# Stationary operands of the float32r matmuls laid out with a stride of two elements

## The reference, cut to what matters

```python
h = rmsnorm(x, lw['norm1_w']) * (1.0 + scale1) + shift1
proj = jnp.einsum('btd,dc->btc', h, lw['w_in'])            # 1024 -> 2304
...
s = jnp.einsum('bkgqd,bskd->bkgqs', qblk, k) * scale       # attention scores
p = jax.nn.softmax(s, axis=-1)
o = jnp.einsum('bkgqs,bskd->bkgqd', p, v)                  # attention values
...
out = jnp.einsum('btc,cd->btd', jnp.concatenate([att, ret], axis=-1), lw['w_out'])
...
gates, idx = lax.top_k(aff.transpose(0, 2, 1), cap)        # experts choose tokens
a = jnp.einsum('becd,edf->becf', xg, lw['w_gate'])
u = jnp.einsum('becd,edf->becf', xg, lw['w_up'])
y = jnp.einsum('becf,efd->becd', jax.nn.silu(a) * u, lw['w_down'])
```

## Time before, and the profile before

| | us |
|---|---|
| median of 3 runs | 3144.37 |
| lowest and highest of them | 3141.43, 3145.56 |
| the profiled execution | 3139.49 |
| its span, first to last instruction | 3137.8 |
| PE busy | 2974.2 |
| PEld busy | 2739.5 |
| DVE busy | 1852.7 |
| ACT busy | 1674.1 |
| POOL busy | 700.5 |

### The profile page before, as it was taken

How to read it: one execution, slowest core, us unless ns; L and a number is a source line. 1 busy time by engine, 2 the same in 40 slices (tenths; PEclk the granted TensorE clock), 3 DMA queues, 4 the chain that set the end, 5 groups by cost and what they waited for, 6 DMA issues and landing times. The chain is left out here.

```text
span 3137.8 us, 57856 instructions
## 1 busy us (share of the span) xinstructions
PE 2974.2 (95%) x20880; PEld 2739.5 (87%) x20880; DVE 1852.7 (59%) x3261; ACT 1674.1 (53%) x3227; POOL 700.5 (22%) x878
## 2 busy tenths in 40 slices
PE   8999997899999999999899969999999999999996
PEld 5888886688888888888788759999999999999996
DVE  5222225788888888888643387655555555555555
ACT  4222223677777777777534336544444454454454
POOL 1333335632323223232000011111111111111104
PEclk9999999999999999999899959999999999999998
DMA  7211116501010010010164336666666666666657
GB/s 256 84 68 68 68 60 203 178 14 35 17 30 20 17 33 17 20 30 17 45 208 148 120 96 201 188 194 189 194 197 189 196 196 189 191 199 195 194 184 285
DMA packets 320130, 394.76 MB, mean 126 GB/s; under 512 B 30260, under 2 KB 276488, under 8 KB 319016
## 3 DMA queue, kind: packets, MB, share of 16 engines
q1 hardware_dynamic: 307416, 356.18, 34.5%
q0 software_dynamic: 12240, 36.77, 4.8%
q10 hardware_dynamic: 384, 0.62, 0.1%
HBM read 319.60 MB, written 74.06 MB: 125 GB/s over the span
## 5 line engine op out<-in xcount | busy, mean ns | idle before, releaser
L2877 DVE TENSOR_TENSOR e_w_lo<-e_raw,e_w_hi 128x2048 fp32r<-128x2048 f32 x189 | 433.1, 2291 | 411.7 <-ACT e_w_hi L2794 411.7
L92 PE MATMUL e_ps<-e_x_hi,e_w_hi 128*128 128x272 f32 x2048 | 601.6, 294 | 2.6 <-issue 2.6
L94 PE MATMUL e_ps<-e_x_hi,e_w_lo 128*128 128x272 f32 x2048 | 593.4, 290 | 0.0
L93 PE MATMUL e_ps<-e_x_lo,e_w_hi 128*128 128x272 f32 x2048 | 590.0, 288 | 0.0
L1709 DVE TENSOR_TENSOR a_pT_lo<-a_ps_t,a_pT_hi 128x512 fp32r<-128x512 f32 (+1 forms) x648 | 367.8, 600 | 137.2 <-ACT a_pT_hi L1618 136.9
L1618 ACT ACTIVATE a_pT_hi<-a_ps_t 128x512 fp32r<-128x512 f32 (+1 forms) x648 | 319.3, 532 | 160.2 <-PE a_ps_t L1486 155.1
L92 PEld LDWEIGHTS e_ps<-e_x_hi,e_w_hi 128*128 128x128 f32 x2048 | 386.3, 189 | 3.0 <-issue 3.0
L93 PEld LDWEIGHTS e_ps<-e_x_lo,e_w_hi 128*128 128x128 f32 x2048 | 387.0, 189 | 0.0
L94 PEld LDWEIGHTS e_ps<-e_x_hi,e_w_lo 128*128 128x128 f32 x2048 | 385.8, 188 | 0.0
L2794 ACT ACTIVATE e_w_hi<-e_raw 128x2048 fp32r<-128x2048 f32 x189 | 360.6, 1908 | 0.0
L1486 PE MATMUL a_ps_t<-ident,a_prob 128*128 128x128 f32 x2184 | 329.6, 280 | 29.9 <-DVE a_pT_lo L1709 19.1
(11 more groups left out here) (358 smaller groups left out, 5492.3 us busy)
## 6 DMA issues: line engine op xcount, KB each, us to landing
e_raw<-in_w_gate SPq DMA_DIRECT2D x64, 1024.0 KB, 5.0
e_raw<-in_w_up SPq DMA_DIRECT2D x64, 1024.0 KB, 5.0
e_raw<-in_w_down SPq DMA_DIRECT2D x64, 1024.0 KB, 5.0
s_ret<-p_pr SPq DMA_DIRECT2D x17, 768.0 KB, 3.6
p_raw<-in_w_in SPq DMA_DIRECT2D x8, 1152.0 KB, 18.7
o_cT<-s_ct SPq DMA_DIRECT2D x17, 512.0 KB, 4.9
s_x<-o_x SPq DMA_DIRECT2D x17, 512.0 KB, 5.0
s_xn<-o_xn SPq DMA_DIRECT2D x17, 512.0 KB, 3.6
```

The source lines that it names most:

```text
L92: nc.tensor.matmul(out, w_hi, x_hi, start=first, stop=False)
L93: nc.tensor.matmul(out, w_hi, x_lo, start=False, stop=False)
L94: return nc.tensor.matmul(out, w_lo, x_hi, start=False, stop=last)
L2877: nc.vector.tensor_tensor(w_lo[n % RING][:, :, :], raw[n % RING][:, :, :], w_hi[n % RING][:, :, :].bitcast(F32), ALU.subtract).then_inc(w_ ...
```

## The change

Five stationary operands change their place in SBUF. Where there were two tiles, for the high and the low part, there is one tile with a last dimension of 2, in which the high part is element 0 and the low part element 1: `p_h`, `o_c` and `e_w`. A view of one part then has its elements 8 bytes apart, where before they were 4 bytes apart. In `a_vals` the high and the low part of a head have to be one operand of 128 columns, and there it is the two key-value heads that are interleaved; the operand of one head again has its elements 8 bytes apart.

```diff
--- before.py
+++ after.py
@@ -130,8 +130,9 @@
             if spare:
                 k.sb(f"p_spare{i}", [P, spare // 4])
-            h_hi.append(k.sb(f"p_hhi{i}", [P, DC, P], F32R))
-            h_lo.append(k.sb(f"p_hlo{i}", [P, DC, P], F32R))
+            pair = k.sb(f"p_h{i}", [P, DC, P, 2], F32R)
+            h_hi.append(pair[:, :, :, 0])
+            h_lo.append(pair[:, :, :, 1])
@@ -1129,7 +1130,7 @@
-            self.vals = k1.sb("a_vals", [P, NTA + 1, NKV, 2, HD], F32R)
+            self.vals = k1.sb("a_vals", [P, NTA + 1, 2, HD, NKV], F32R)
@@ -1399,10 +1400,10 @@
             for v in range(NKV):
-                nc.gpsimd.tensor_copy(vals[:, :, v, 0, :], src[:, :, v, :]).then_inc(vals_ok, 1)
+                nc.gpsimd.tensor_copy(vals[:, :, 0, :, v], src[:, :, v, :]).then_inc(vals_ok, 1)
             for v in range(NKV):
                 pool.wait_ge(vals_ok, v + 1)
-                nc.gpsimd.tensor_tensor(vals[:, :, v, 1, :], src[:, :, v, :], vals[:, :, v, 0, :].bitcast(F32), ALU.subtract)\
+                nc.gpsimd.tensor_tensor(vals[:, :, 1, :, v], src[:, :, v, :], vals[:, :, 0, :, v].bitcast(F32), ALU.subtract)\
                     .then_inc(vals_ok, 1)
@@ -1504,7 +1505,7 @@
                         ins = nc.tensor.matmul(ps_o[:, :, :],
-                                               vals[:, src, grp * GROUP // QPK, :, :].rearrange("p d f -> p (d f)"),
+                                               vals[:, src, :, :, grp * GROUP // QPK].rearrange("p d f -> p (d f)"),
                                                part[grp % 2][:, c, :, :], start=first, stop=last)
@@ -1796,8 +1797,8 @@
-        c_hi = [k.sb(f"o_c_hi{i}", [P, DC, P], F32R) for i in range(2)]
-        c_lo = [k.sb(f"o_c_lo{i}", [P, DC, P], F32R) for i in range(2)]
+        pairs = [k.sb(f"o_c{i}", [P, DC, P, 2], F32R) for i in range(2)]
+        c_hi, c_lo = ([pair[:, :, :, part] for pair in pairs] for part in range(2))
@@ -2461,8 +2462,8 @@
-            self.w_hi = [k1.sb(f"e_w_hi{i}", [P, DC, self.BC], F32R) for i in range(self.RING)]
-            self.w_lo = [k1.sb(f"e_w_lo{i}", [P, DC, self.BC], F32R) for i in range(self.RING)]
+            pairs = [k1.sb(f"e_w{i}", [P, DC, self.BC, 2], F32R) for i in range(self.RING)]
+            self.w_hi, self.w_lo = ([pair[:, :, :, part] for pair in pairs] for part in range(2))
```

## The result

| | before, us | changed, us |
|---|---|---|
| median of 9 runs of each | 3144.37 | 3153.09 |
| lowest and highest | 3140.50, 3148.35 | 3148.66, 3155.02 |
| the profiled execution, span | 3137.8 | 3151.6 |

The ratio is 1.003, 95% interval 1.0022 to 1.0039: the changed kernel is slower by 0.3%, 7 to 12 us. The forecast was 3045 us.

What follows compares the result with a forecast made beforehand. PE was taken to bound the kernel through the gaps between matmul starts. Weight loads gain 100 us, splits and POOL values cost 0: median 3144.4 - 100 = 3044, stated as 3045 us, range 2995 to 3215.

Steps and rivals of the forecast that it cites:

- Step (1): Weight loads of all stages: strided loads collide less with the moving stream, shortening matmul gaps; 100 us gain.
- The upper bound of that step: All matmul stages: gaps shrink to streaming time or the 110 ns of a load, in sum 169 us gain.
- Attention: Value matmuls: at most 6 ns less per gap (13 us), part of it given back to DVE.
- Steps (2) and (3): Strided splits on ACT and DVE, and values on POOL: hidden behind PE or by 12.5 us to spare; cost 0.
- Nothing changes: Every matmul: the excess is a fixed cost of a float32r matmul, whatever is loaded; 3144 us, chance 0.20.
- More lines, more collisions: Every stage: each memory line a load fetches costs the stream, so the excess doubles; 176 us, 3320 us, chance 0.20.
- The load itself becomes slow: Experts and attention: a load takes 220 ns, not 110, and no longer hides; over 4200 us, chance 0.05.
- The splits take over: Experts: slower strided splits on DVE delay PE; 58 us at 0.3 us a block, 3200 us, chance 0.09.

Runs made afterwards that it cites:

- experiment 1: Reference left out, 64 equal float32r matmuls per setting, stride, distance and columns varied: mean gap for 512 columns 232.0 ns at stride 1, 232.1 at stride 2.
- the bench: Kernels that leave out the whole reference and time 64 equal matmuls per setting, nothing beside them; 512 columns at stride 1, distance 0: 226.7 ns.
- experiment 7: Kernel before, experts' moving tiles laid out to fix the distance, no stride: 3118.45 us (0.9931) at 64 bytes, 3147.80 us (1.0017) at 128.
- experiment 3: Reference left out, stride 1, moving operand shifted in 32-byte steps against two stationary places: sixteen pairs of equal distance agree within 0.8 ns.
- experiment 8: Projection's stationary tiles moved by 64 bytes: in the kernel before 3148.21 us (1.0020), in the changed kernel 3146.61 us (1.0016 to before).

## Why the prediction was wrong

**What bounds the kernel.** Right: PE in every stage of weight, and the gaps between starts as its pace. Also right that the excess depends on addresses; the distance in the experts runs through four values, one for each chunk, and with the distance held fixed the gaps of all chunks are alike (nearly all between 122 and 125 ns at 64, where they were spread from 120 to 130). The two pairs of 0.13 and 0.12 us in the earlier trace rows could not show this by themselves, since most gaps of 126 ns are rounded to one of the two.

**Step (1), the weight load, failed.** Its sentence was that a load beside a stream "slides past it and collides on the way, and at 4 bytes in a cycle it would keep its distance and collide seldom". The term was 100 us of gain, and it was worth a loss of 11.6 us over the four stretches. Neither moving the load's address faster nor reading fewer columns removes the excess (experiment 1). In its place the runs show a gap that goes by distance, width and stride together. The change left the distances as they were (but for the low parts, and the values of the second key-value head, which stand 4 bytes on) and drew another number for each stage: for the projection, which stood at its best place of those tried, +9.2 ns in the row shown and +7.2 over the stage; for the output projection +5.0; for the experts, which go through four places, -0.6 and -0.5; for the values +4 and +3.5. The upper bound of that step was out of reach too: no setting of the bench came under 226.7 ns for 512 columns or 123.3 for 272, 13 and 10 ns above the stream.

**Attention.** The step said that part of what changes there would be taken up by DVE. It held in the other direction: the gaps between value matmuls that follow each other grew by 7.2 us in sum (237.2 to 244.4), and the stretch by 0.4 us. From the last value matmul of a run to the transposes behind it, where PE waits, the sum fell by 4.2 us (46.1 to 41.9). PE's busy time rose by 3.8 us, from 885.0 to 888.8, and its idle time fell from 44.6 to 41.2. With the others strided only, the stretch was 931.6 us, 2.0 more.

**Steps (2) and (3)** were right in cost, 0, and in cover. ACT's split grew by 0.17 us a block; PE needs 6 us for one. Not foreseen was that ACT would be slower at all and DVE not.

**The rivals.** "Nothing changes" was nearest in time (3144), but wrong in its mechanism: the excess is not fixed, as experiment 7 shows at 24 us. The rule of the Trainium skill that step (1) weighed, of loads and streams with ports of their own (TensorE: Matmul & The Clock Gate, Part 2, Step-by-step), came nearer to the time than my reading, but it can't be the whole of it: the gap goes by how the two operands stand to each other (experiment 3). "More lines, more collisions" had the sign of the result but not its cause: it would make the experts slower too, and they became faster. "The load itself becomes slow" does happen, at stride 4, though not at 2. (The prediction put its threshold at 15%, the experts' room; in attention a load had only 6 ns to spare, as it says itself, so 5% would have cost something there.) "The splits take over" did not occur.

**The range**, 2995 to 3215 us, held the time, in its upper half, and not by the reading that gave the forecast; the chance of 0.46 for a faster kernel stood on the failed step.

**What stays open.** Why a distance gives its gap is not shown: the excess is often 32 cycles, belongs to float32r, and goes with both addresses, which looks like two readers of one memory falling into step, but no run separates the port from the engine's own sequence. Nor is it known what puts the changed projection into the cycle of 235.5 ns in place of 233.0 (end of experiment 8). Its low parts, at 4 bytes modulo 32, a distance that the bench had not, do not explain it by themselves: they stand the same in tiles 1 and 15, and in the output projection, which has them too, the mean is 232.9 ns.

## What to carry to other kernels

When matmuls follow each other without a pause and still cost more than their columns, time a row of equal ones at several distances between the two operands before a layout is changed: here a small bench gave the gaps of most stages to about a nanosecond, with one miss of 4 ns, and less closely where the distance changes from chunk to chunk, and a spare of 192 bytes with a wider row for the moving tiles was worth 24 us, more than any stride. A stage whose operands already stand at the best place, as the projection's did, has nothing to gain by a change of layout and something to lose, so each stage has to be looked at by itself. An excess that looks alike in two stages is no sign of a fixed cost: vary one quantity before it is put into a sum.

## What the runs showed of the hardware that I had not expected

- A float32r matmul with its load takes 10 to 21 ns above its columns in the bench at strides 1 and 2 (in the kernel 7 ns at the least, for 256 columns at distance 64); a bfloat16 one 2.5 ns, at any distance and stride tried.
- That excess depends on the distance of the stationary from the moving operand modulo 256 bytes, by up to 7.6 ns for 512 columns and 3.4 for 272 at stride 1, and not on either address alone.
- The same float32r matmuls at the same addresses ran at 233.0 ns in one tile and at 235.5 in another.
- The load's row is 188 ns for contiguous float32r columns, 196 at 8 bytes, 310 at 16, and 109 for 32 columns in place of 128; the gap for 512 columns follows only the third of these.
- ACT writes 2048 float32r elements at 8 bytes apart in 2080 ns in place of 1908; DVE reads one such operand and writes the other in 2295 ns in place of 2291.
